# Entries above 128 tokens: weights stationary with 160 to 256 tokens streamed, gathers in groups of 32 tokens, scatters in steps of 16 rows

## What is computed

```python
N_EXPERTS = 64; TOP_K = 8; D_FF_EXPERT = 256      # D_MODEL = 1024, t = 1024 tokens
_, idx = lax.top_k(masked, TOP_K)                  # 8 experts of each token
wts = take_along_axis(scores, idx); wts = wts / sum(wts) * ROUTE_SCALE
# the 8192 assignments are sorted by expert, and padded to blocks; for a block of expert e:
xb = h_pad[rt]                                     # the block's tokens
hid = jax.nn.silu(xb @ w1[e]) * (xb @ w3[e])       # (tokens, 256)
ob = (hid @ w2[e]) * rw[:, None]                   # (tokens, 1024)
y = y.at[rt].add(ob)
```

## Time and profile before

| | us |
|---|---|
| median of 3 runs | 2463.86 |
| the profiled execution | 2483.54 |
| its span | 2481.8 |
| PE busy in the span | 2401.2 |
| DVE busy | 1182.6 |
| POOL busy | 640.1 |
| ACT busy | 482.6 |

### The profile page before, as it was taken

How to read it: one execution, slowest core, us unless ns; L and a number is a source line. 1 busy time by engine, 2 the same in 40 slices (tenths; PEclk the granted TensorE clock), 3 DMA queues, 4 the chain that set the end, 5 groups by cost and what they waited for, 6 DMA issues and landing times.

```text
span 2481.8 us, 32549 instructions
## 1 busy us (share of the span) xinstructions
PE 2401.2 (97%) x8544; PEld 1174.5 (47%) x8545; DVE 1182.6 (48%) x2744; ACT 482.6 (19%) x892; POOL 640.1 (26%) x653
## 2 busy tenths in 40 slices
PE   6999999999999999999999999999999999999996
PEld 3444444555544556566444554444444444444442
DVE  3376222666655666666244766433333333343332
ACT  3311000444431133332211121200000000000000
POOL 0000000000021100000211235555454545455551
PEclk9999999999999999999999999999999999999998
DMA  8231334342373133221444214589899999999995
GB/s 259 50 71 44 81 72 128 110 134 92 123 191 80 52 81 94 94 72 61 132 132 125 95 43 179 180 291 295 280 302 332 317 317 335 312 364 344 326 335 126
DMA packets 122933, 437.49 MB, mean 176 GB/s; under 512 B 22205, under 2 KB 24461, under 8 KB 97121
## 3 DMA queue, kind: packets, MB, share of 16 engines
q1 hardware_dynamic: 78208, 306.91, 35.9%
q0 software_dynamic: 44640, 129.49, 19.8%
HBM read 369.72 MB, written 73.93 MB: 179 GB/s over the span
## 4 chain that ended last, share of the span: by engine, by line
PE 84%; DVE 7%; another core or an unknown queue 4%; issue 2%; DMA 1%; ACT 1%; SPq 1%; POOL 0%; DVEq 0%; ACTq 0%; POOLq 0%
PE psum L992 21%; PE psum L1474 17%; PE psum L1077 8%; PE psum L1541 8%; PE psum L1323 7%; PE psum L1340 3%; PE psum L1479 3%; PE psum L1280 2%; PE psum L1547 2%; PE psum L1384 2%; PE psum L1148 2%; PE psum L1158 2%; PE psum L1167 1%; PE psum L1407 1%
## 5 line engine op out<-in xcount | busy, mean ns | idle before, releaser
L992 PE MATMUL psum<-mem 128*128 128x512 f32 x1536 | 689.7, 594 | 1.0 <-DMA mem<-in_w_in 0.8
L1474 PE MATMUL psum<-mem 128*128 x1008 | 449.9, 594 | 1.7 <-DVE mem L2685 1.2
L992 PEld LDWEIGHTS psum<-mem 128*128 128x128 f32 x1536 | 279.2, 191 | 293.6 <-issue 290.5
L785 POOL DMA_INDIRECT mem<-h_d,idx x312 | 316.4, 1014 | 360.3 <-DVE idx L2766 255.4
L1474 PEld LDWEIGHTS psum<-mem 128*128 128x128 f32 x1008 | 186.4, 190 | 230.0 <-issue 230.0
L2744 DVE TENSOR_TENSOR mem<-mem,psum 128x256 f32<-128x256 f32 x93 | 39.1, 421 | 457.2 <-ACT mem L1953 344.0
L1541 PE MATMUL psum<-mem 128*128 128x512 f32 x504 | 229.8, 603 | 15.0 <-ACT mem L1956 13.6
L1077 PE MATMUL psum<-mem 128*128 128x512 f32 x448 | 192.8, 592 | 0.0
L790 POOL DMA_INDIRECT out_x<-mem,put x93 | 142.1, 1527 | 90.5 <-issue 72.3
L1323 PE MATMUL psum<-mem 128*128 128x512 f32 x384 | 165.0, 592 | 0.0
L1541 PEld LDWEIGHTS psum<-mem 128*128 128x128 f32 x504 | 93.4, 191 | 141.0 <-issue 141.0
(11 more groups left out here) (421 smaller groups left out, 2483.1 us busy)
## 6 DMA issues: line engine op xcount, KB each, us to landing
mem<-in_exp_w SPq DMA_DIRECT2D x201, 1024.0 KB
mem<-in_w_in SPq DMA_DIRECT2D x16, 2048.0 KB, 14.4
proj_d<-mem SPq DMA_DIRECT2D x104, 256.0 KB, 2.0
mem<-in_ada_w POOLq DMA_DIRECT2D x16, 1024.0 KB, 6.2
mem<-proj_d POOLq DMA_DIRECT2D x56, 256.0 KB, 3.0
mem<-proj_d POOLq DMA_DIRECT2D x20, 512.0 KB, 5.7
mem<-in_ada_w SPq DMA_DIRECT2D x4, 2048.0 KB, 23.2
mem<-in_w_branch SPq DMA_DIRECT2D x3, 2048.0 KB, 8.2
```

Of the source, the lines that this page charges most:

```text
L785: g.indirect_dma_start(x[:, 2 * P * n:2 * P * (n + 1)], None, h2_q, bass.IndirectOffsetOnAxis(ap=idx[:, p, j, n:n + 1], axis=0), bounds_ch ...
L992: mm = t.matmul(bank(unit_bank(u)), l, r, start=(k == 0), stop=(k == KD - 1))
L1474: return t.matmul(bank(up_banks[j][r]), xgT[r][:, k, P * j:P * (j + 1)], up_piece(h, r, k), start=(k == 0), stop=(k == KD - 1))
```

## The change

**Wide entries, PE.** With `n > 128` the up products have the *weights stationary*. For each half `f` of the 256 hidden values, each of the two matrices `z` and each k, a 128x128 piece of `w1` or `w3` is loaded (every second column, a stride of 8 bytes), and 160, 192, 224 or 256 tokens stream through (`up_wide`). These are 32 products for an entry, 15 before the place of `turn_hidden` and 17 after it. The results stand with hidden values on the partitions, as `downs` needs them. Each width, each of four buffers and each of the two parts has its own code, chosen by branches (`by_width`, `If(h > 0)`). `up_second` is gone, and so are `turn_tile` and `turn_half_tile` of a wide entry; PE still waits for `e_hid[1]` at that place.

**Wide entries, DVE and ACT.** `hidden` writes straight to `hidT`, twice for an entry as before. ACT no longer copies for a wide entry.

**Gathers.** `fetch_tile` issues one gather for each started group of 32 tokens. DVE's `turn_rows` has branches for 1 to 4 groups.

**Scatters.** The row count is chosen in steps of 16 by nested branches (`by_rows`), 8 ends where there were 4.

```diff
+            def up_wide(b, f, z, k, n):
+                w = w13[b][:, z, k, :].rearrange("p (n f) -> p f n", f=FK)[:, f, :]
+                return t.matmul(psum[:, up_banks[f][b % 2], 2 * P * z:2 * P * z + n], w, xgT[b % 2][:, k, 0:n],
+                                start=(k == 0), stop=(k == KD - 1))
...
-            def up_half_second(b):
+            def up_wide_begin(b, n):
                 for k in range(KD):
-                    mm = up_half(1, b, k)
+                    up_wide(b, 0, 0, k, n)
+                for k in range(KD - 1):
+                    up_wide(b, 0, 1, k, n)
+
+            def up_wide_end(b, n):
+                up_wide(b, 0, 1, KD - 1, n).then_inc(e_H[0], 1)
+                for z in range(2):
+                    for k in range(KD):
+                        mm = up_wide(b, 1, z, k, n)
                 mm.then_inc(e_H[1], 1)
 
+            def by_width(n, part, b):
+
+                with pe.If(n > P + HALF):
+                    with pe.If(n > P + HALF + 32):
+                        part(b, 2 * P)
+                    with pe.Else():
+                        part(b, P + HALF + 32)
...
             def up_begin(n, h, r):
 
                 with pe.If(n > HALF):
-                    for k in range(UP_AHEAD):
-                        up(0, h, r, k)
+                    with pe.If(n > P):
+                        with pe.If(h > 0):
+                            by_width(n, up_wide_begin, 2 + r)
+                        with pe.Else():
+                            by_width(n, up_wide_begin, r)
+                        pe.nop()
+                    with pe.Else():
+                        for k in range(UP_AHEAD):
+                            up(h, r, k)
+                    pe.nop()
...
             def downs(n, p, loads, now):
                 pe.wait_ge(e_v[p], loads)
                 pe.wait_ge(e_ob[0], now)
-                pe.wait_ge(e_hc[0], now)
                 with pe.If(n > HALF):
                     with pe.If(n > P):
                         down_second(n, p)
+                    with pe.Else():
+                        turned.wait(e_hc)
...
             def fetch_tile(n, j, p):
-                gather(xg[j][p], j, p, (0, 1), e_xg[j][p])
-                with pool.If(n > P * j + HALF):
-                    gather(xg[j][p], j, p, (2, 3), e_xg[j][p])
+                gather(xg[j][p], j, p, (0,), e_xg[j][p])
+                with pool.If(n > P * j + 32):
+                    gather(xg[j][p], j, p, (1,), e_xg[j][p])
+                    with pool.If(n > P * j + HALF):
+                        gather(xg[j][p], j, p, (2,), e_xg[j][p])
...
+            def by_rows(n, low, high, act):
+
+                if high - low == 16:
+                    act(high)
+                    return
+                middle = (low + high) // 2
+                with pool.If(n > middle):
+                    by_rows(n, middle, high, act)
+                with pool.Else():
+                    by_rows(n, low, middle, act)
...
             def hidden_rows(n, now, p):
-                dve.wait_ge(e_si[0], now)
-                hidden(0, p)
                 with dve.If(n > P):
+                    dve.wait_ge(e_si[0], now)
+                    hidden(hidT[p][:, 0, :], 0, p)
                     wide.up()
                     wide.wait(e_si[1])
-                    hidden(1, p)
+                    hidden(hidT[p][:, 1, :], 1, p)
+                with dve.Else():
+                    dve.wait_ge(e_si[0], now)
+                    hidden(hid, 0, p)
```

More of the change, by code:

```diff
@@ L213, in layer_kernel @@
         hidT = [view(23040 + 512 * p, FK, 2 * P) for p in range(2)]
-        hid = [view(24064 + 256 * j, FF) for j in range(2)]
+        hid = view(24064, FF)
         idx = sb("idx", [P, 2, 2, 4], I32)
@@ L342, in layer_kernel @@
         e_xg = [two("xg0"), two("xg1")]
-        e_H, e_si, e_hid, e_hT, e_hc, e_O, e_ob = (two(n) for n in ("H", "si", "hid", "hT", "hc", "O", "ob"))
+        e_H, e_si, e_hid, e_O, e_ob = (two(n) for n in ("H", "si", "hid", "O", "ob"))
+        e_hT, e_hc = sem("e_hT"), sem("e_hc")
         e_w += [sem(f"e_w{b}") for b in (2, 3)]
@@ L845, in ready, with add @@
                     pool.sem_inc(e_go, 1)
[L847 to L863, removed]
+                    scatter_tile(1, p, rows - P)
+                by_rows(n, P, 2 * P, add)
             def add_first(n, p, weighed):
-                def ready():
+                def add(rows):
                     added.wait(e_sc)
@@ L871, in ready @@
                     pool.sem_inc(e_go, 1)
[L873 to L889, removed]
+                    scatter_tile(0, p, rows)
+                by_rows(n, 0, P, add)
             def add_rows(n, p, weighed):
@@ new lines, in by_width @@
+            def by_width(n, part, b):
[6 more added lines that the diff above has]
+                with pe.Else():
+                    with pe.If(n > P + 32):
+                        part(b, P + HALF)
+                    with pe.Else():
+                        part(b, P + 32)
+                    pe.nop()
+                pe.nop()
@@ L1512, in up_end @@
                 with pe.If(n > HALF):
-                    for k in range(UP_AHEAD, KD):
-                        mm = up(0, h, r, k)
-                    mm.then_inc(e_H[0], 1)
+                    with pe.If(n > P):
+                        seconds.up()
+                        with pe.If(h > 0):
+                            by_width(n, up_wide_end, 2 + r)
+                        with pe.Else():
+                            by_width(n, up_wide_end, r)
+                        pe.nop()
+                    with pe.Else():
+                        for k in range(UP_AHEAD, KD):
+                            mm = up(h, r, k)
+                        mm.then_inc(e_H[0], 1)
+                    pe.nop()
                 with pe.Else():
@@ L1953, in silu, with hidden_turned @@
                 s.activation(sg[:, j, :], bank(up_banks[j][p])[:, 0:FF], ACT.Silu).then_inc(e_si[j], 1)
[L1955 to L1956 removed]
+            def hidden_turned(p, n):
+                s.activation(hidT[p][:, :, 0:n], psum[:, 1, 0:2 * n].rearrange("p (f n) -> p f n", f=FK), ACT.Copy).then_inc(e_hc, 1)
             act.wait_ge(s_ya, NT - 1)
             act.wait_ge(s_tab, 1)
[L1960 removed]
+            for x in (*e_si, e_hc):
                 act.sem_inc(x, 1)
[L1962 removed]
+            wide, narrow = Count(act, "wide"), Count(act, "narrow")
             def act_item(it, q):
@@ L1975, in act_item @@
                 act.sem_inc(e_up, 1)
-                with act.If(n > HALF):
-                    with act.If(n > P):
-                        wide.wait(e_hT[1])
-                        hidden_turned(0, q % 2, P)
-                        with act.If(n > P + HALF):
-                            hidden_turned(1, q % 2, P)
-                        with act.Else():
-                            hidden_turned(1, q % 2, HALF)
-                        act.nop()
+                with act.If(n <= P):
+                    narrow.up()
+                    with act.If(n > HALF):
+                        narrow.wait(e_hT)
+                        hidden_turned(q % 2, P)
                     with act.Else():
-                        act.wait_ge(e_hT[0], now)
-                        hidden_turned(0, q % 2, P)
+                        narrow.wait(e_hT)
+                        hidden_turned(q % 2, HALF)
                     act.nop()
-                with act.Else():
-                    act.wait_ge(e_hT[0], now)
-                    hidden_turned(0, q % 2, HALF)
                 act.nop()
@@ L2677, in _ @@
             dve.wait_ge(e_clear, 1)
-            got = [[Count(dve, f"got{j}{p}", 0, 32) for p in range(2)] for j in range(2)]
+            got = [[Count(dve, f"got{j}{p}", 0, 16) for p in range(2)] for j in range(2)]
             def turn_group(j, p, groups):
-                for _ in range(groups // 2):
+                for _ in range(groups):
                     got[j][p].up()
```

110 lines of the change are left out of this document (56 added, 54 removed).

## The result

The changed kernel takes 3334.25 us (median of 4 runs, 3326.52 to 3341.78) against 2463.87 us before, a ratio of 1.3532 with a 95% interval of 1.3515 to 1.3548. It is 870 us slower (the two profiled executions lie 843 us apart, as that of the kernel before took 2483.5 us). The forecast was 2597 us and its range ended at 2830 us: the direction and its cause were right, and the loss was more than six times the 133 us forecast.

What follows compares the result with a forecast made beforehand. PE was taken to bound the loop, DMA close behind. Refetched code made a round 12 + 7 x 2.64 = 30.5 us, 991 us in all, 133 more than 858: 2463.9 + 133 = 2597 us, range 2415 to 2830 us.

Steps and rivals of the forecast that it cites:

- What bounds the kernel: Loop over the entries: PE bounds it, busy 97 to 98 of 100 us, with DMA close behind.
- That the code would decide: PE's loop, 977 to 2,743 instructions: fetched again each round, 133 us more; slower by code fetch had chance 0.60.
- How many packets a round: PE's loop: a round enters about 8 blocks, so some 7 to 8 packets a round, 230 to 260 in all.
- The price of a wait: PE's branches into absent blocks: 2.64 us each, the mean of 2.07 and 3.21 us, with 7 waits a round.
- The sequencer's own time: PE's loop: 12 us a round besides the waits, from some 60 branches and register steps at 0.20 us.
- The PE part of the sum: PE's loop, if nothing else happens: 22.6 + 16.8 + 10 = 49 us sooner, at most 55.
- Streaming: Wide entries' up products: 64 passes at 0.84 ns a column with weight loads hidden, 22.6 us gained.
- the rivals at 0.178 and 0.190 us: Wide up products: strided loads or loads set the pass, 4 us won or 7 us lost; within no change, 0.06.
- Transposes: Wide entries on PE: 91 transposes go, each 0.185 us, together 16.8 us.
- ACT's copies: PE's waits for ACT before down products: between 0 and 15.5 us go, taken as 10.
- The wait for `e_hid[1]`: PE's wait between wide entries' up products, behind 15 of 32 products: put at nothing.
- Gathers and scatters: 312 gathers become 287, output rows 9184 become 8640; 2.9% less traffic, worth nothing by itself as PE is the limit.

Runs made afterwards that it cites:

- e7: The changed kernel with wide entries streaming 192 or 256 tokens only, plus 131 never-executed instructions ahead of the loop: 2466.29 us, ratio 0.9964.
- e8: The kernel before with only the change's gather groups, row turns and 16-row scatter steps, PE's program unchanged: 2472.27 us, ratio 0.9987.
- e3: The kernel before with four never-executed stretches of 54 matmuls for each r, a loop of 2721 instructions: 3391.13 us, ratio 1.366.
- e11: e7 again, unchanged, on another chip: 2451.01 us, ratio 0.9955 to the kernel before.
- e5: The kernel before with never-executed stretches of 18 matmuls, a loop of 1569 instructions: 2485.77 us, ratio 1.0041.
- e9: The kernel before with never-executed stretches of 23 matmuls (loop of 1729 instructions) and 131 unused instructions ahead of the loop: 2482.54 us, ratio 1.0077.
- e6: The kernel before with never-executed stretches of 10 matmuls, a loop of 1313 instructions: 2485.63 us, ratio 1.004.
- e1: The changed kernel with wide entries streaming 192 or 256 tokens only, a loop of 1671 instructions: 2963.15 us, ratio 1.1943.

## Why the prediction was wrong in size

**What bounds the kernel**: right. PE is the bound before and in e7, and e8 with its 3 us says the same of DMA.

**That the code would decide**: right, and shown by e3 and e7. The Trainium skill, "Runtime: NRT & Kernel Launch", section "Instruction fetch mechanics", had pointed there, with 2048 instructions as PE's store. The runs agree that a loop of more than that is fetched anew. They are stricter: a loop of 1697 instructions was fetched too, and 7 touched blocks are the most that stayed. The same section speaks of a window of two pages, outside of which a taken branch waits; the prediction took the whole store for that window. By two pages every loop here would be fetched in each round; those over 5 to 7 blocks were not. Whether an eighth block is taken by what is fetched ahead, no row shows.

The forecast for a round was 12 + 7 x 2.64 = 30.5 us, and 52.5 us were measured. Of the 22 us between them 8.6 stand in the waits and 13.4 beside them; the slower clock, 213/32.5 = 6.6 us a round, is in these 22.

**How many packets a round**: the first failed step. I counted about 8 blocks that a round *enters*. Measured are 13.3 packets, for a loop of 10.7 blocks. A block is fetched whether its code runs or not: e3 adds only code that never runs, and pays for all of it. Over the five kernels it is the loop's length in blocks plus 2.5 to 2.8. What this surplus is, the traces do not say. The number of waits held: branches over 1 us were 6.4 a round, near my 7. The times of the packets show where the others went. Of the 433, 307 landed while one of the 208 long branches ran: 108 branches took in two packets each, 91 one, 9 none. The other 126, 3.9 a round, landed outside of them.

**The price of a wait**: the second failed step. I took 2.64 us from the loop's first two waits, as if one wait were one packet. The mean in the loop is 882/208 = 4.24 us, up to 7.76 us. Branches with one packet took 3.9 us in the mean, those with two 4.8 us. Seven waits at 2.64 us are 18.5 us a round; 6.4 at 4.24 us are 27.1 us. My upper bound, 3.21 us, was the larger of only two samples.

**The sequencer's own time**: the third failed step, and the largest. I had 12 us a round besides the waits, and 52.5 - 27.1 = 25.4 us are measured. The short branches are 5.9 us of it (191 us in 32.5 rounds). The rest I take for fetches in straight code, and for time in which the sequencer stood behind PE's own work; no run separates the two. I had assumed that the work would lie wholly beside the waits. It did so in part only: while branches of over 1 us ran, PE was idle for 470 of their 882 us. The other 412 us were covered by matmuls that had been issued.

**The clock**: missing. There was no term for it, though an engine that stands for 6 us at a time and then runs at half its rate is in no row of the kernel before. It is 213 us of busy time here, a quarter of the loss. It is some 15 us more if one counts that the work itself had become less: at a granted clock of 0.99 PE is busy for 822.5 us in e11's loop, and at 1.00 for 837.7 us in that of the kernel before.

**The PE part of the sum, by e7 against e8.** Both are from the same batch. The up products of the entry with 17 tokens, early in the loop, start at (timeline of PE, e7 and then e8):

```profile
1665.39 3.84 PE L1468 MATMUL psum<-mem 128*64 128x256 f32 x32
```

```profile
1649.83 2.48 PE L1467 MATMUL psum<-mem 128*64 128x256 f32 x20
```

and those of the entry with 180 tokens, 49 entries on:

```profile
2293.24 5.04 PE L1474 MATMUL psum<-mem 128*128 128x192 f32 x30
```

```profile
2300.26 4.46 PE L1462 MATMUL psum<-mem 128*128 x10
```

e7 is 15.6 us late at the first and 7.0 us early at the second: it gains 22.6 us on the way, over 20 wide entries. The terms there:

- *Streaming*: as predicted. 30 passes of 192 columns in 5.04 us are (5.04 - 0.33)/29 = 0.162 us each, for a calculated 0.161. The changed kernel shows 0.136 us for 160 columns (below, 30 passes in 4.24 us) and 0.189 us for 224. So the weight loads are hidden even at 160 columns, though one is 197 ns long; the rivals at 0.178 and 0.190 us fall. The stride isn't what made L1580's loads longer than L1584's either: in e7 the strided loads last 197 ns and the unstrided ones at L1463 192 ns.

```profile
1817.39 4.24 PE L1474 MATMUL psum<-mem 128*128 128x160 f32 x30
```

  With two widths the 8 entries up to 192 tokens give 3.9 us, and the 12 others cost 1 us.
- *Transposes*: too dear in the forecast. 0.74 us for four includes the tail of the last one. In the full-tile place of the kernel before two of them take 1819.49 - 1819.27 = 0.22 us from start to start:

```profile
1819.27 0.39 PE L1580 MATMUL psum<-ident,mem 128*128 128x128 f32 x2
1819.49 0.27 PE L1584 MATMUL psum<-ident,mem 128*128 128x128 f32 x1
1819.61 9.61 PE L1474 MATMUL psum<-mem 128*128 x22
```

  So 0.11 us each, and 0.17 us behind short entries. For the 72 on this way it is 8 to 12 us; for all 91 it is 10 to 15 us instead of 16.8.
- *ACT's copies*: the wait before the full down products, and its successor, over the whole loop, in e8 and in e7:

```profile
L1529 PE MATMUL psum<-mem 128*128 128x512 f32 x502 | 227.2, 599 | 7.8 <-ACT mem L1944 7.0 <-issue 0.6
```

```profile
L1553 PE MATMUL psum<-mem 128*128 128x512 f32 x504 | 229.3, 602 | 3.3 <-issue 2.9
```

  The wait for ACT is gone, 7 us. It was 13.6 us in the earlier trace rows. The groups didn't take the difference: e5, with the old ones, has 6.4 us for ACT here. It varies between executions.

That makes 18 to 22 us, and 22.6 were measured. **What the sum lacked** is the way into the loop. The longer loop has to be fetched once, and PE stands meanwhile. In e7:

```profile
1587.61 7.13 PE L1463 MATMUL psum<-mem 128*128 x16 [2.64 <-issue]
1598.96 6.84 PE L1463 MATMUL psum<-mem 128*128 x10 [4.22 <-issue]
...
1607.75 2.84 PE L1463 MATMUL psum<-mem 128*128 x6 [1.72 <-issue]
```

These waits are 8.6 us, and the 10 passes at 1598.96 take 6.84 us instead of 4.46. The queue brought 7 packets between 1580 and 1612 us, where the kernel before had 4:

```profile
q8 instruction: 7, 0.11, 1.4%
```

Against e8, e7 is 2.0 us late at PE's last products ahead of the loop and 11.6 us at the first down products (1610.43 against 1598.81 us), so the way in costs it 9.6 us. e9 shows that this is the code and not the new products. It has PE's old work and also brings 7 packets:

```profile
1581.67 3.70 PE L1407 MATMUL psum<-mem 128*128 128x512 f32 x8 [0.47 <-ACT mem L1931]
...
1598.48 7.51 PE L1474 MATMUL psum<-mem 128*128 x10 [4.66 <-issue]
```

Its first down products start at 1610.10 us, and its way in is 8.9 us longer than e8's.

The way in isn't all of the 15.6 us. Two entries on, e7 is 8.8 us late, and one wide entry raises that to 15.7 us. In it PE stands between single passes, 3.7 us in all, and the clock falls. The first such passes, and the same entry in e11:

```profile
1648.02 0.38 PE L1474 MATMUL psum<-mem 128*128 128x256 f32 x1 [0.42 <-issue]
1648.75 0.38 PE L1474 MATMUL psum<-mem 128*128 128x256 f32 x1 [0.35 <-issue]
1650.87 0.38 PE L1474 MATMUL psum<-mem 128*128 128x256 f32 x1 [1.75 <-issue]
```

```profile
1648.31 7.51 PE L1474 MATMUL psum<-mem 128*128 128x256 f32 x34
```

e11 is the same kernel on another chip and has nothing of the kind. It is 9.4 us late at the first point and 16.6 us early at the second, against the same e8, so it gains 26 us on the way. Behind the second point e7 gives back 2.4 us, in part here:

```profile
2298.34 5.97 PE L1474 MATMUL psum<-mem 128*128 128x192 f32 x34
2305.99 5.40 PE L1553 MATMUL psum<-mem 128*128 128x512 f32 x8 [1.67 <-issue]
```

The down products came 1.67 us too late, and the 8 passes took 5.40 us where they take 3.60. e11 has no idle time at this place, and 0.2 us before all its full down products together. What holds e7 up in these places, no run shows.

*The wait for `e_hid[1]`*, put at nothing: right. PE's group behind it in e7 has 0.7 us of idle time in all, over 832 passes of 192 columns:

```profile
L1474 PE MATMUL psum<-mem 128*128 128x192 f32 x832 | 140.4, 327 | 0.7 <-issue 0.7
```

**Gathers and scatters**: right. There are 287 gathers, and the saved traffic is worth 3 to 5 us.

**The range** failed because its upper end was made from a price seen twice in a first round and a count of entered blocks, with the sequencer's own time fixed at 12 us and no term for the clock.

## What to carry to other kernels

Count PE's instructions in a loop before writing out more variants, and where the blocks of 256 fall. Below the edge an unused variant costs little (256 instructions more made no difference between e6 and e5), and 28 instructions past it cost a fetch of every block in every round, used or not. Here that is 15 us on a round of 26 us. If a loop stands just over the edge, move it or drop the variant that gains least; and price the first pass of new code, which here took 9 to 10 us of what the new products gave.

## What the runs showed of the hardware

- Seven touched blocks of 256 instructions stayed on PE, with up to 1729 instructions; eight, with 1671, did not. The blocks are counted, not seen. There is no gentle slope: 131 instructions that are never executed took e1's 19% loss away (e7).
- Fetched code made a round 1.6 to 2.1 us longer for each packet of 16 KB, also where the code was never run. A long branch ended 1.4 us (median) after the last packet that landed in it.
- The granted clock fell 88 times in the loop of the changed kernel. The last idle time that began before a fall was 4.8 us long in the median, and passes of 512 columns then took 0.85 us instead of 0.43. A stall of the sequencer is paid twice.
- Loads of 128x128 weights with a stride of two values stay hidden under passes of 160 columns: 0.136 us a pass (the change).
